# Gate weights of both layers and the context's output weights copied in memory, and loaded from the copies

## The chip, the cores and the metric

The kernel runs on one NeuronCore of one Trainium2 chip, in one launch. The metric is the device time in microseconds. A core has a matrix engine (TensorE, in the profile PE), a vector engine (DVE), a scalar engine (ACT), GpSimd (POOL) and a queue engine (SyncE, SP), which run side by side and meet at semaphores. 16 DMA engines move data between the device memory and the on-chip memory (SBUF). A transfer is issued by SP, ACT or POOL and is cut into packets, each a run of bytes that is contiguous on both sides. SP and ACT issue to hardware queues (q1 in the page), POOL to a software queue (q0).

## The reference

Two layers of a trunk over 256 latent tokens with 256 context tokens, width 1024, all in float32. What matters here:

```
pc = modulate(xc, norm1, sh1_c, sc1_c) @ w_in        # 6832 columns, the last 4096 of them gate logits
pl = modulate(xl, norm1, sh1_l, sc1_l) @ w_in
...                                                  # four mixers: two attentions, mLSTM, Hyena
def merge_branches(ys, gate_logits, w_branch, w_out):
    gl = gate_logits.reshape(B, L, N_BRANCH, -1)
    acc = sigmoid(gl[:, :, 0]) * (ys[0] @ w_branch[0])
    for i in range(1, N_BRANCH):
        acc = acc + sigmoid(gl[:, :, i]) * (ys[i] @ w_branch[i])
    return acc @ w_out
xl = xl + g1_l * merge_branches(..latents..)
xc = xc + g1_c * merge_branches(..context..)         # in the first layer alone
xc, xl = both + g2 * peer(modulate(both, norm2, ..)) # 8 heads x 16 of 16384 experts for each token
```

`w_in` and `w_out` are stored row by row, so a chunk of 256 columns is 1024 runs of 1 KB. The gate columns of one layer are 16 such chunks (16 MB), `w_out` is 4.

## The kernel before

The program is a row of stages with a barrier of all engines between them: `begin`, `opening` (line 2374), `experts_beside` (line 2489), `closing`, `experts` and `store`. `opening` does the first layer's context keys and the whole of its latent stream up to the residual. `experts_beside` does the first layer's experts for all 512 tokens, which fetch 128 rows of 4 KB from each of two tables for every token by indirect transfers that POOL issues, and weaves two strings of other work in between: first the context's own first layer (with its gates and its output product), then the second layer's latent projections, gates and Hyena. `closing` and `experts` finish the second layer.

A stage is a list of parts. A part has ticks, and in each tick methods for some engines (`sync` for SP, `tensor` for TensorE and so on). The stage's plan is one list of (part, tick); `perform` walks it once for each engine, so every engine runs its own instructions in the plan's order, and an instruction that waits holds up everything behind it on that engine. `braid` interleaves strings of ticks in proportion to their lengths.

`Gates` (line 1499) computes the gate logits: 32 tiles of 128 columns, two in a chunk. `Gates.load` (line 1518) is SP's load of chunk c into one of two ring buffers; from chunk 2 on it waits until TensorE is done with chunk c - 2 (`mult`). The tile's eight products stand at line 1556. `Branches` (line 1598) computes 32 steps of `ys @ w_branch`, two products each (line 1647), with eight chunks of 512 KB for four steps each, loaded at line 1616 two chunks ahead. `Merged` (line 1675) is the output product (line 1713) with four chunks of `w_out`, loaded at line 1691; its first two loads are issued at its first tick.

The second half of the opening's plan (lines 2421 to 2423; `g` are the gates' ticks, `b` the branches'):

```python
plan += braid(whole(attn), whole(conv), g[14:22])
plan += braid(whole(lstm), g[22:], b[:16])
plan += b[16:] + braid(whole(merged), whole(other))
```

Hyena's first tick (line 1387) makes SP load `k_dft` and the stored spectra, 1 MB each. Each kind of part has its own semaphores; transfers that SP issues go out in SP's order. In `experts_beside` the context's gates, its output product and the second layer's gates use a ring whose buffers are 256 columns wide, so that the eight pieces of a chunk lie one behind the other in each SBUF partition (8 KB).

Of the kernel before, what the change touches and what calls it, by code (L numbers as in the profile page):

```python
# [12 lines left out]
F32 = mybir.dt.float32  # L13
# [6 lines left out]
P = 128  # L20
D = 1024
KD = D // P
# [18 lines left out]
O_GATE = O_HY + 3 * HY_W  # L41
# [30 lines left out]
def sbuf(nc, name, shape, dtype):  # L72

    NUMBER[1] += 1
    return nc.sbuf_tensor(f"{name}_{NUMBER[1]}", shape, dtype)


class Chain:


    def __init__(self, eng, sem):
        self.eng, self.sem, self.n = eng, sem, 0
# [178 lines left out]
class Part:  # L261
# [3 lines left out]
    after = ()  # L265
# [5 lines left out]
    def sync(self, sp, i):  # L271
        pass
# [14 lines left out]
def whole(part):  # L287
    return [(part, i) for i in range(part.ticks)]


def braid(*strings):

    at = [((j + 0.5) / len(s), n, x) for n, s in enumerate(strings) for j, x in enumerate(s)]
    return [x for _, _, x in sorted(at, key=lambda a: a[:2])]
# [48 lines left out]
class Modulation(Part):  # L343
# [3 lines left out]
    STEPS = 9  # L347
# [1148 lines left out]
STEPS = [(i, k) for i in range(N_BRANCH) for k in range(KD)]  # L1496


class Gates(Part):
# [2 lines left out]
    LOT = 4  # L1502
    ticks = len(STEPS) + 2

    def __init__(self, nc, sems, m, w_in, f, ring, sig, banks, after, branches, room=None, flip=0, away=None):
        self.away = away
        self.room_for, self.flip = room if room else [after, after], flip
        self.nc, self.m, self.f, self.ring, self.sig, self.banks, self.after = nc, m, f, ring, sig, banks, after
        self.w = w_in.rearrange("(k p) n -> p k n", p=P)
        self.branches, self.room = branches, sig.shape[1]  # L1510
        self.mult, self.out, self.sigmoids, self.in0, self.in1, *self.stored = sems(
            "g_mult", "g_out", "g_sigmoids", "g_in0", "g_in1", *([f"g_stored{j}" for j in range(2)] if away is not None else []))
        self.ins = [self.in0, self.in1]
# [4 lines left out]
    def load(self, sp, c):  # L1518
        if c >= 2:
            sp.wait_ge(self.mult, 2 * (c - 1))  # L1520
        else:
            for sem, n in self.room_for[c]:
                sp.wait_ge(sem, n)
        at = O_GATE + 256 * c
        sp.dma_start(self.ring[:, (c + self.flip) % 2, :, 0:256], self.w[:, :, at:at + 256]).then_inc(self.ins[c % 2], 16)

    def sync(self, sp, i):
        if i == 0:
# [31 lines left out]
    def scalar(self, act, i):  # L1560
        nc, j, L = self.nc, i - 1, self.LOT
        if 0 <= j < len(STEPS):
            if j == 0:
                self.enter(act)
            act.wait_ge(self.mult, j + 1)
            if j >= self.room and self.away is None:
                act.wait_ge(self.branches.prod_done, j - self.room + 1)
            elif j >= self.room and j % self.LOT == 0:
                lot = (j - self.room) // self.LOT
                act.wait_ge(self.stored[lot % 2], 16 * (lot // 2 + 1))  # L1570
            nc.scalar.copy(self.sig[:, j % self.room, :], self.m.ps[:, self.banks[j % 2], 0:T]).then_inc(self.out, 1)  # L1571
        if i >= 2 and (i - 1) % L == 0:
            act.wait_ge(self.out, i - 1)
            at = (i - 1 - L) % self.room
            nc.scalar.activation(self.sig[:, at:at + L, :], self.sig[:, at:at + L, :], ACT.Sigmoid
                                 ).then_inc(self.sigmoids, 1)


class Fetched(Part):
# [95 lines left out]
class Merged(Part):  # L1675
# [1 line left out]

    ticks = KD + 1

    def __init__(self, nc, sems, m, mod, w_out, acc, ring, lo, banks, after, room):  # L1680
        self.nc, self.m, self.mod, self.acc, self.ring, self.lo, self.banks, self.after = (
            nc, m, mod, acc, ring, lo, banks, after)
        self.w = w_out.rearrange("(k p) n -> p k n", p=P)
        self.kind, self.room = (1 if lo < CTX else 0), room
        self.mult, self.out, *self.ins = sems("o_mult", "o_out", "o_in0", "o_in1")
        self.done = [(self.out, KD)]

    def load(self, sp, c):
        if c >= 2:
            sp.wait_ge(self.mult, 2 * (c - 1))  # L1690
        sp.dma_start(self.ring[:, c % 2, :, 0:256], self.w[:, :, c * 256:(c + 1) * 256]).then_inc(self.ins[c % 2], 16)

    def sync(self, sp, i):
        if i == 0:
# [679 lines left out]
def opening(nc, m, d, l, kv, spectra, rounds, front):  # L2374
# [3 lines left out]
    with sbuf(nc, "arena", [P, X + 12416 - FRONT], F32) as rest, sbuf(nc, "gbias", [1, T + 16], F32) as gbias:  # L2378
        arena = front, rest
        sems = Sems(nc)  # L2380
        f = front_memory(arena)
        vec, mod = m.vec[l], m.mod[l]
        ring, w_in = cut(arena, RING, 2, KD, 272), d["w_in"][l]
# [13 lines left out]
        side = Modulation(nc, sems, m, rounds, cut(arena, MODR, 2, 2, MROUND), cut(arena, MODR + 4096, MCH), 7)  # L2397
# [4 lines left out]
        attn = Attention(nc, sems, m, f, kv, 1, attention_memory(arena, X), (2, 3, 4), heads.done + heads_c.done)  # L2402
        conv = Hyena(nc, sems, m, vec, d, f, hyena_memory(arena, X + 2096, X + 4144), spectra, (5, 6, 7),
                     heads.done + rest1.done)
        lstm = Mlstm(nc, sems, m, vec, f, kv, 1, mlstm_memory(arena, X, NB), (2, 3, 4, 5), attn.done + conv.done)
        branch = Branches(nc, sems, m, d["w_branch"][l], f, cut(arena, MODR, 2, 2, 512), cut(arena, X + LSTM, KD, T),
                          cut(arena, X + LSTM + 2048, 2, T), (6, 7), attn.done + conv.done,
                          [attn.done, attn.done, lstm.done, conv.done], rest1.done)
# [4 lines left out]
                        [(branch.acc_done, len(STEPS)), (gates.mult, len(STEPS))] + lstm.done,  # L2413
                        [(gates.mult, len(STEPS))])
        other = Norm(nc, sems, m, mod, 0, 0, f.h, cut(arena, 2048, T), 4, merged.after, True)
        g, b, q = whole(gates), whole(branch), whole(side)
        plan = braid(whole(norm_c), q[:8])
        plan += whole(proj_c)[:1] + whole(Ahead(proj)) + braid(whole(proj_c)[1:], whole(norm), whole(filt), q[8:24])
        plan += braid(whole(heads_c), whole(proj), q[24:54])
        plan += braid(whole(heads), g[:14], q[54:]) + [(rest0, 0), (rest1, 0)]  # L2420
        plan += braid(whole(attn), whole(conv), g[14:22])
        plan += braid(whole(lstm), g[22:], b[:16])
        plan += b[16:] + braid(whole(merged), whole(other))
        perform(nc, sems, plan)


# [62 lines left out]
def experts_beside(nc, m, d, l, kv, spectra, sigs, front):  # L2489
# [3 lines left out]
    with ExitStack() as ctx:  # L2493
# [3 lines left out]
        sems = Sems(nc)  # L2497
        f = front_memory(arena)
# [11 lines left out]
        branch = Branches(nc, sems, m, d["w_branch"][l], f, cut(arena, 6144, 2, 2, 512), cut(arena, 4096, KD, T),  # L2510
                          cut(arena, Z + 7168, 2, T), (6, 7), conv.done, [[], [], [], []])
        gates = Gates(nc, sems, m, d["w_in"][l], f, cut(arena, Z, 2, KD, 256), cut(arena, Z + 4096, 12, T), (4, 5),
                      conv.done, branch)
        branch.gates = gates
        merged = Merged(nc, sems, m, mod, d["w_out"][l], branch.acc, cut(arena, Z, 2, KD, 256), 0, (4, 5),
                        [(branch.acc_done, len(STEPS)), (gates.mult, len(STEPS)), (gates.out, len(STEPS))],
                        [(gates.mult, len(STEPS))])
        norm2c = Norm(nc, sems, m, mod, 3 * KD, 0, h2, cut(arena, 2048, T), 6,
                      merged.done + [(peer.q_mult, 16), (peer.h_turned, 4)])
        peer.normed = [norm2l, norm2c]  # L2520
# [10 lines left out]
                            known, known)  # L2531
        heads_n = Heads(nc, sems, m, vec, d, l + 1, f, kv, 1, True, True, heads_memory(arena, Z), (6, 7), proj_n.done)
        gates_n = Gates(nc, sems, m, d["w_in"][l + 1], f, cut(arena, Z, 2, KD, 256), cut(arena, Z + 4096, 12, T), (4, 5),
                        heads_n.done, None, away=sigs)
        conv_n = Hyena(nc, sems, m, vec, d, f, hyena_memory(arena, 0, Z), spectra, (4, 5, 6),
                       [(gates_n.mult, len(STEPS)), (gates_n.out, len(STEPS))] + [
                           (gates_n.stored[j], 64) for j in range(2)])
# [19 lines left out]
def build(nc, d, out):  # L2557
    NUMBER[:] = [0, 0]
    m = Mem()
    kv = Mem()  # L2560
    with ExitStack() as ctx:
        sb = lambda name, shape: ctx.enter_context(sbuf(nc, name, shape, F32))
        m.ps = ctx.enter_context(nc.psum_tensor("ps", [P, BANKS, BANK], F32))
        m.sq = sb("squares", [P, C_N, P])
        m.resid = sb("resid", [P, KD, TOK])
        m.cond = sb("cond", [P, KD, 32])
        m.vec = [sb("vec", [P, V_ROWS]) for _ in range(LAYERS)]
        m.mod = [sb("mod", [P, 6 * KD, 2]) for _ in range(LAYERS)]
        m.products = [sb("mod_products", [P, 6 * KD, 2]) for _ in range(LAYERS)]
        m.eps = sb("eps", [P, 1])  # L2570
        kv.km, kv.vm = sb("km", [P, MLA_H, TOK]), sb("vm", [P, NB, MLA_H * MLA_V])
        kv.gk, kv.gv = sb("gk", [P, TOK]), sb("gv", [P, NB, P])
        kv.mk, kv.mv, kv.mg = sb("mk", [P, 2, TOK]), sb("mv", [P, NB, ML_H, HD + 1]), sb("mg", [P, NB, 4 * ML_H])
        spectra = nc.dram_tensor("spectra", (P, 4 * KF * HY_W), F32, kind="Internal").ap()
        begin(nc, m, kv, d)
        rounds = [(d["ada_w"][0], r * MROUND, m.products[0]) for r in range(2, 6)]
        rounds += [(d["ada_w"][1], r * MROUND, m.products[1]) for r in range(6)]
        sigs = nc.dram_tensor("sigs", (P, len(STEPS), T), F32, kind="Internal").ap()
        with sbuf(nc, "front", [P, FRONT], F32) as front:
            opening(nc, m, d, 0, kv, spectra, rounds, front)  # L2580
            experts_beside(nc, m, d, 0, kv, spectra, sigs, front)
            closing(nc, m, d, 1, kv, sigs, front)
        experts(nc, m, d, 1)
        store(nc, m, out)
# [99 lines left out]
```

## Time and profile before

| | |
|---|---|
| median of 3 runs | 3312.9 us (3311.84 to 3319.93) |
| the profiled execution | 3324.62 us, span 3322.7 us |
| TensorE, DVE, POOL, ACT busy | 2296.2, 1849.8, 1748.8, 617.3 us |
| moved | 1028.53 MB, mean 310 GB/s |
| software queue (q0), hardware queue (q1) | 847.35 MB and 179.15 MB, 66.8% and 16.1% of 16 engines' span |
| packets | 395065; under 2 KB 176283, under 8 KB 393755 |

The profile covers one execution. The span is from its first to its last instruction. The opening lasts until about 573 us, `experts_beside` until about 2310, `closing` until about 2570. A transfer's landing is counted from its issue by the queue's engine to the arrival of its last byte's semaphore. A queue's share is the time that its packets took, summed over 16 engines, over 16 times the stretch.

### The profile page before, as it was taken

How to read it: one execution, taken by the hardware profiler on the slowest of the kernel's cores; microseconds unless marked ns; L12 is line 12 of the kernel's file. 1: busy time of each engine (PE TensorE's matmuls, PEld its weight loads, DVE VectorE, ACT ScalarE, POOL GpSimd, SP SyncE). 2: the span in 40 equal slices, each digit the busy share in tenths (PEclk: the TensorE clock that was granted, in tenths of full speed). 3: DMA queues.
4: the chain of work that ended last, by engine and by line, in shares of the span. 5: the costliest groups of instructions: out<-in, count | busy, mean ns of one | idle time of the engine just before them, and what ended most of it. 6: DMA issues, size and time to landing. Idle time of an engine off the chain costs nothing. (4 is left out here: it accounts for less than half of the span.)

```text
span 3322.7 us, 31994 instructions
## 1 busy us (share of the span) xinstructions
PE 2296.2 (69%) x10877; PEld 1372.8 (41%) x10877; DVE 1849.8 (56%) x4792; ACT 617.3 (19%) x1252; POOL 1748.8 (53%) x1580
## 2 busy tenths in 40 slices
PE   5999999878857787566676477554798555444435
PEld 3676687734525555123443155321576322101001
DVE  1324334667775556767446945573334766666652
ACT  2113531124211121112102112210241111110000
POOL 0001000467675566777667666776000577777775
PEclk8999999877668898667888688866789766555555
DMA  8576223899999999999999999998303999999997
GB/s 293 178 266 236 88 64 105 298 335 382 333 379 337 350 391 368 383 385 352 349 349 384 334 354 396 401 386 332 113 7 113 307 387 405 403 386 383 395 367 312
DMA packets 395065, 1028.53 MB, mean 310 GB/s; under 512 B 31891, under 2 KB 176283, under 8 KB 393755
## 3 DMA queue, kind: packets, MB, share of 16 engines
q0 software_dynamic: 232064, 847.35, 66.8%
q1 hardware_dynamic: 162794, 179.15, 16.1%
q8 instruction: 89, 1.46, 0.2%
q14 instruction: 70, 0.57, 0.0%
q10 hardware_dynamic: 48, 0.01, 0.0%
HBM read 1019.05 MB, written 7.34 MB: 309 GB/s over the span
## 5 line engine op out<-in xcount | busy, mean ns | idle before, releaser
L1885 POOL DMA_INDIRECT expert_rows<-in_peer_u,chosen x768 | 867.2, 1129 | 850.1 <-DVE chosen L2241 576.8
L2133 DVE CUSTOM_DVE_ANT_0 expert_rows<-expert_rows,h_rows 128x1024 f32<-128x1024 f32 x768 | 935.9, 1222 | 554.6 <-DMA expert_rows<-in_peer_u,chosen 532.3
L1898 POOL DMA_INDIRECT expert_rows<-in_peer_v,row_of x768 | 852.5, 1110 | 410.9 <-PE ps L2025 210.3
L2025 PE MATMUL ps<-expert_rows,weights 128*32 128x512 f32 x3072 | 589.7, 849 | 685.4 <-DMA expert_rows<-in_peer_v,row_of 682.9
L2025 PEld LDWEIGHTS ps<-expert_rows,weights 128*32 128x32 f32 x3072 | 77.2, 125 | 963.3 <-issue 953.7
L1556 PE MATMUL ps<-front,arena 128*128 128x256 f32 x1536 | 384.8, 408 | 79.3 <-DMA arena<-in_w_in 78.5
L1556 PEld LDWEIGHTS ps<-front,arena 128*128 128x128 f32 x1536 | 308.7, 205 | 163.3 <-DMA arena<-in_w_in 63.9
L595 PE MATMUL ps<-front,arena 128*128 128x256 f32 (+1 forms) x816 | 201.9, 406 | 43.6 <-DMA arena<-in_w_in 39.5
L1953 PE MATMUL ps<-h,wq 128*128 128x256 f32 x768 | 200.4, 415 | 5.1 <-ACT h L439 3.7
L595 PEld LDWEIGHTS ps<-front,arena 128*128 128x128 f32 (+1 forms) x816 | 159.7, 199 | 89.2 <-issue 34.1
L361 POOL DMA_DIRECT2D arena<-in_ada_w x40 | 28.8, 719 | 285.0 <-PE ps L384 246.4
L1953 PEld LDWEIGHTS ps<-h,wq 128*128 128x128 f32 x768 | 155.7, 210 | 54.3 <-issue 30.6
L1571 ACT COPY arena<-ps 128x256 f32<-128x256 f32 x96 | 35.9, 373 | 330.7 <-PE ps L1556 330.7
L1647 PE MATMUL ps<-front,arena 128*128 128x256 f32 x256 | 65.0, 402 | 16.0 <-DVE arena L1663 12.4
L2098 ACT COPY weights<-ps 128x128 f32<-128x128 f32 x48 | 12.8, 266 | 337.7 <-DVE row_of L2176 266.9
L2076 ACT ACTIVATE gelu<-dots 128x16 f32<-128x16 f32 x48 | 10.4, 216 | 344.4 <-DVE dots L2133 344.2
L2058 ACT COPY scores<-ps 128x256 f32<-128x256 f32 x48 | 17.8, 372 | 297.3 <-PE ps L1967 297.3
L629 DVE COPY front<-ps 128x256 f32<-128x256 f32 (+2 forms) x28 | 11.8, 422 | 109.0 <-PE ps L595 99.6
L943 DVE TENSOR_REDUCE arena<-ps 128x1 f32<-128x512 f32 (+1 forms) x48 | 28.8, 600 | 74.3 <-PE ps L893 73.9
L831 DVE RECIPROCAL arena<-arena 96x512 f32<-96x512 f32 (+2 forms) x21 | 63.9, 3042 | 10.9 <-ACT arena L741 10.4
L2043 ACT COPY subkeysT<-ps 128x256 f32<-128x256 f32 x48 | 17.8, 371 | 266.9 <-PE ps L1932 266.9
L1186 DVE SCALAR_TENSOR_TENSOR arena<-arena,ps 128x256 f32<-128x256 f32 x80 | 25.5, 376 | 69.1 <-PE ps L1075 59.9
(356 smaller groups left out, 3185.6 us busy)
## 6 DMA issues: line engine op xcount, KB each, us to landing
arena<-in_w_in SPq DMA_DIRECT2D x79, 1024.0 KB, 13.5
arena<-in_ada_w POOLq DMA_DIRECT2D x40, 1024.0 KB, 6.5
wq<-in_peer_wq SPq DMA_DIRECT2D x48, 512.0 KB, 9.4
arena<-in_w_out SPq DMA_DIRECT2D x12, 1024.0 KB, 7.7
expert_rows<-in_peer_u,chosen POOLq DMA_INDIRECT x768, 6.6
expert_rows<-in_peer_v,row_of POOLq DMA_INDIRECT x768, 7.1
ada_w<-in_ada_w SPq DMA_DIRECT2D x4, 2048.0 KB, 23.0
arena<-in_w_branch SPq DMA_DIRECT2D x16, 512.0 KB, 3.5
```

What stands on the lines that cost most here:

```text
L361: pool.dma_start(self.raw[:, j % self.RING, :, :], weights.rearrange("(k p) n -> p k n", p=P)[:, k0:k0 + 2, lo:lo + MROUND]).then_inc(self ...
L595: ins = nc.tensor.matmul(m.ps[0:n, bank, 0:T], w, h[:, k, :], start=(k == 0), stop=(k == KD - 1))
L831: self.own.link(nc.vector.reciprocal(self.tile(x.rs2, j), self.tile(x.rs2, j)))
L943: self.own.link(nc.vector.reduce_max(x.st[:, 2, u:u + 1], m.ps[:, self.S, 0:n], axis=AX.X))
L1556: ins = nc.tensor.matmul(m.ps[:, self.banks[i % 2], 0:T], self.ring[:, (c + self.flip) % 2, k, (i % 2) * P:(i % 2 + 1) * P], self.f.h[:, k ...
L1571: nc.scalar.copy(self.sig[:, j % self.room, :], self.m.ps[:, self.banks[j % 2], 0:T]).then_inc(self.out, 1)
L1647: ins = nc.tensor.matmul(m.ps[:, self.bank(n), 0:T], self.wb[:, n // 4 % 2, a, (k % 4) * P:(k % 4 + 1) * P], self.f.yT[:, i, a, :], start= ...
L1885: nc.gpsimd.indirect_dma_start(x.ring[:, j % self.R, :], None, self.u_rows, bass.IndirectOffsetOnAxis(x.chosen[:, w, q:q + 1], 0)).then_in ...
L1898: nc.gpsimd.indirect_dma_start(x.ring[:, j % self.R, :], None, self.v_rows, bass.IndirectOffsetOnAxis(x.rows[:, w % 4, 4 * c + r:4 * c + r ...
L1953: ins = nc.tensor.matmul(m.ps[:, self.QB + c, 0:T], x.wq[:, b, part, k, c * P:(c + 1) * P], self.h[:, 4 * part + k, :], start=(part == 0 a ...
L2025: ins = nc.tensor.matmul(m.ps[to:to + 32, half, :], flat[:, r * P + 32 * c:r * P + 32 * c + 32], x.ring[:, self.place_of["v", a] % self.R, ...
L2133: nc.vector.tensor_tensor_reduce(u, u, x.ht, 1.0, 0.0, ALU.mult, ALU.add, x.dots[:, at:at + 1]).then_inc(self.u_dotted, 1)
```

## The change

A new part, `Relay`, issues on SP 36 copies from memory to memory: the 16 gate chunks of layer 0, the 4 chunks of layer 0's `w_out` and the 16 gate chunks of layer 1. Each copy reads a chunk as it lies in the weights (1024 runs of 1 KB) and writes it to a new tensor in device memory in which each partition's part of a chunk is 8 KB in one run. A copy waits for nothing; at the last tick SP waits until all 36 have landed. The ticks are braided into the second half of the opening: 18 with attention and Hyena, 10 with mLSTM, 8 with the last branch steps. In `experts_beside` the context's gates, its output product and the second layer's gates load from the new tensors. The opening's own gates and output product, and the closing's, load as before.

```diff
--- before.py
+++ after.py
@@ -1502,8 +1502,8 @@
     LOT = 4
     ticks = len(STEPS) + 2
 
-    def __init__(self, nc, sems, m, w_in, f, ring, sig, banks, after, branches, room=None, flip=0, away=None):
-        self.away = away
+    def __init__(self, nc, sems, m, w_in, f, ring, sig, banks, after, branches, room=None, flip=0, away=None, flat=None):
+        self.away, self.flat = away, flat
         self.room_for, self.flip = room if room else [after, after], flip
         self.nc, self.m, self.f, self.ring, self.sig, self.banks, self.after = nc, m, f, ring, sig, banks, after
         self.w = w_in.rearrange("(k p) n -> p k n", p=P)
@@ -1522,7 +1522,8 @@
             for sem, n in self.room_for[c]:
                 sp.wait_ge(sem, n)
         at = O_GATE + 256 * c
-        sp.dma_start(self.ring[:, (c + self.flip) % 2, :, 0:256], self.w[:, :, at:at + 256]).then_inc(self.ins[c % 2], 16)
+        weights = self.w[:, :, at:at + 256] if self.flat is None else self.flat[c]
+        sp.dma_start(self.ring[:, (c + self.flip) % 2, :, 0:256], weights).then_inc(self.ins[c % 2], 16)
 
     def sync(self, sp, i):
         if i == 0:
@@ -1574,6 +1575,24 @@
             at = (i - 1 - L) % self.room
             nc.scalar.activation(self.sig[:, at:at + L, :], self.sig[:, at:at + L, :], ACT.Sigmoid
                                  ).then_inc(self.sigmoids, 1)
+
+
+class Relay(Part):
+
+
+
+    LOTS = 4
+
+    def __init__(self, sems, copies):
+        self.copies, self.ticks = copies, len(copies)
+        self.copied = sems(*[f"copied{j}" for j in range(self.LOTS)])
+
+    def sync(self, sp, i):
+        to, src = self.copies[i]
+        sp.dma_start(to, src).then_inc(self.copied[i % self.LOTS], 16)
+        if i == self.ticks - 1:
+            for j in range(self.LOTS):
+                sp.wait_ge(self.copied[j], 16 * len(range(j, self.ticks, self.LOTS)))
 
 
 class Fetched(Part):
@@ -1677,7 +1696,8 @@
 
     ticks = KD + 1
 
-    def __init__(self, nc, sems, m, mod, w_out, acc, ring, lo, banks, after, room):
+    def __init__(self, nc, sems, m, mod, w_out, acc, ring, lo, banks, after, room, flat=None):
+        self.flat = flat
         self.nc, self.m, self.mod, self.acc, self.ring, self.lo, self.banks, self.after = (
             nc, m, mod, acc, ring, lo, banks, after)
         self.w = w_out.rearrange("(k p) n -> p k n", p=P)
@@ -1688,7 +1708,8 @@
     def load(self, sp, c):
         if c >= 2:
             sp.wait_ge(self.mult, 2 * (c - 1))
-        sp.dma_start(self.ring[:, c % 2, :, 0:256], self.w[:, :, c * 256:(c + 1) * 256]).then_inc(self.ins[c % 2], 16)
+        weights = self.w[:, :, c * 256:(c + 1) * 256] if self.flat is None else self.flat[c]
+        sp.dma_start(self.ring[:, c % 2, :, 0:256], weights).then_inc(self.ins[c % 2], 16)
 
     def sync(self, sp, i):
         if i == 0:
@@ -2413,14 +2434,14 @@
                         [(branch.acc_done, len(STEPS)), (gates.mult, len(STEPS))] + lstm.done,
                         [(gates.mult, len(STEPS))])
         other = Norm(nc, sems, m, mod, 0, 0, f.h, cut(arena, 2048, T), 4, merged.after, True)
-        g, b, q = whole(gates), whole(branch), whole(side)
+        g, b, q, c = whole(gates), whole(branch), whole(side), whole(Relay(sems, m.copies))
         plan = braid(whole(norm_c), q[:8])
         plan += whole(proj_c)[:1] + whole(Ahead(proj)) + braid(whole(proj_c)[1:], whole(norm), whole(filt), q[8:24])
         plan += braid(whole(heads_c), whole(proj), q[24:54])
         plan += braid(whole(heads), g[:14], q[54:]) + [(rest0, 0), (rest1, 0)]
-        plan += braid(whole(attn), whole(conv), g[14:22])
-        plan += braid(whole(lstm), g[22:], b[:16])
-        plan += b[16:] + braid(whole(merged), whole(other))
+        plan += braid(whole(attn), whole(conv), g[14:22], c[:18])
+        plan += braid(whole(lstm), g[22:], b[:16], c[18:28])
+        plan += braid(b[16:], c[28:]) + braid(whole(merged), whole(other))
         perform(nc, sems, plan)
 
 
@@ -2510,11 +2531,11 @@
         branch = Branches(nc, sems, m, d["w_branch"][l], f, cut(arena, 6144, 2, 2, 512), cut(arena, 4096, KD, T),
                           cut(arena, Z + 7168, 2, T), (6, 7), conv.done, [[], [], [], []])
         gates = Gates(nc, sems, m, d["w_in"][l], f, cut(arena, Z, 2, KD, 256), cut(arena, Z + 4096, 12, T), (4, 5),
-                      conv.done, branch)
+                      conv.done, branch, flat=m.flat[0])
         branch.gates = gates
         merged = Merged(nc, sems, m, mod, d["w_out"][l], branch.acc, cut(arena, Z, 2, KD, 256), 0, (4, 5),
                         [(branch.acc_done, len(STEPS)), (gates.mult, len(STEPS)), (gates.out, len(STEPS))],
-                        [(gates.mult, len(STEPS))])
+                        [(gates.mult, len(STEPS))], m.flat[1])
         norm2c = Norm(nc, sems, m, mod, 3 * KD, 0, h2, cut(arena, 2048, T), 6,
                       merged.done + [(peer.q_mult, 16), (peer.h_turned, 4)])
         peer.normed = [norm2l, norm2c]
@@ -2531,7 +2552,7 @@
                             known, known)
         heads_n = Heads(nc, sems, m, vec, d, l + 1, f, kv, 1, True, True, heads_memory(arena, Z), (6, 7), proj_n.done)
         gates_n = Gates(nc, sems, m, d["w_in"][l + 1], f, cut(arena, Z, 2, KD, 256), cut(arena, Z + 4096, 12, T), (4, 5),
-                        heads_n.done, None, away=sigs)
+                        heads_n.done, None, away=sigs, flat=m.flat[2])
         conv_n = Hyena(nc, sems, m, vec, d, f, hyena_memory(arena, 0, Z), spectra, (4, 5, 6),
                        [(gates_n.mult, len(STEPS)), (gates_n.out, len(STEPS))] + [
                            (gates_n.stored[j], 64) for j in range(2)])
@@ -2576,6 +2597,13 @@
         rounds = [(d["ada_w"][0], r * MROUND, m.products[0]) for r in range(2, 6)]
         rounds += [(d["ada_w"][1], r * MROUND, m.products[1]) for r in range(6)]
         sigs = nc.dram_tensor("sigs", (P, len(STEPS), T), F32, kind="Internal").ap()
+        m.flat = [[], [], []]
+        m.copies = []
+        for j, (w, at, n) in enumerate(((d["w_in"][0], O_GATE, 16), (d["w_out"][0], 0, 4), (d["w_in"][1], O_GATE, 16))):
+            flat = nc.dram_tensor(f"flat{j}", (n, P, KD * 256), F32, kind="Internal").ap()
+            for c in range(n):
+                m.flat[j].append(flat[c].rearrange("p (k n) -> p k n", k=KD))
+                m.copies.append((m.flat[j][c], w.rearrange("(k p) n -> p k n", p=P)[:, :, at + 256 * c:at + 256 * (c + 1)]))
         with sbuf(nc, "front", [P, FRONT], F32) as front:
             opening(nc, m, d, 0, kv, spectra, rounds, front)
             experts_beside(nc, m, d, 0, kv, spectra, sigs, front)
```

## Rows read from the trace of the kernel before

**Rows 1.** The page's slices: 40 equal parts of the span, busy tenths.

```profile
PE   5999999878857787566676477554798555444435
...
DMA  8576223899999999999999999998303999999997
```

**Rows 2.** Table by stretch, with granted clock, DMA share, GB/s.

```profile
core 0: us, PE busy (x) PEld busy (x) DVE busy (x) ACT busy (x) POOL busy (x), PEclk, DMA share, GB/s
330.00:560.00 230.00, 216.48 (x1097) 171.62 (x1098) 91.75 (x262) 83.49 (x170) 0.00 (x0) 0.97 0.25 80
...
1010.00:1330.00 320.00, 255.66 (x1195) 176.51 (x1195) 182.59 (x493) 56.12 (x98) 191.12 (x172) 0.88 0.98 364
...
1890.00:2150.00 260.00, 182.98 (x872) 119.51 (x872) 138.56 (x371) 49.23 (x83) 176.99 (x150) 0.85 1.00 379
...
1270.00:1290.00 20.00, 16.25 (x82) 10.62 (x80) 16.75 (x45) 1.66 (x2) 11.90 (x12) 0.99 1.04 395
```

**Rows 3.** Waits of 330 to 560 us on TensorE: us in total, times, longest.

```profile
PE ps L893 <- ACT arena L921: 4.8, 6, 1.9
```

**Rows 4.** DMA view of 1100 to 1330 us: packets, MB, share; issues to landing.

```profile
q1 hardware_dynamic: 18607, 19.53, 25.2%
...
arena<-in_w_in SPq DMA_DIRECT2D x10, 1024.0 KB, 17.4
```

**Rows 5.** DMA view of 2363 to 2372 us.

```profile
DMA packets 491, 3.63 MB, mean 403 GB/s; under 512 B 48, under 2 KB 48, under 8 KB 48
...
q1 hardware_dynamic: 491, 3.63, 98.6%
```

**Rows 6.** Waits in 1010 to 1335 and in 1890 to 2155 us, all engines.

```profile
PE ps L1556 <- DMA arena<-in_w_in: 32.8, 8, 12.8
...
PE ps L1556 <- DMA arena<-in_w_in: 45.7, 12, 15.4
```

**Rows 7.** DMA view of 333 to 338 us, 40 slices, 1 KB packets first.

```profile
GB/s 360 385 369 385 393 385 385 385 393 385 377 352 319 287 311 303 401 320 533 492 508 393 393 524 328 393 459 393 524 328 393 459 393 524 262 590 197 418 238 254
```

**Rows 8.** DMA view of 343 to 352 us: one load alone.

```profile
q1 hardware_dynamic: 1040, 1.05, 38.1%
...
arena<-in_w_in SPq DMA_DIRECT2D x1, 1024.0 KB, 5.2
```

**Rows 9.** The two loads of line 1691 between 530 and 533 us.

```profile
L1691 SPq DMA_DIRECT2D arena<-in_w_out x2: 469/526/582, 531.4 to 531.9; - x2
...
DMA to landing us min/median/max: 6.3/7.5/8.7
```

**Rows 10.** SP's timeline in the opening: start us, us, issue.

```profile
330.61 0.37 SPq L1387 DMA_DIRECT2D arena<-in_k_dft  x1
...
421.78 14.06 SPq L1525 DMA_DIRECT2D arena<-in_w_in  x2
...
523.74 0.37 SPq L1616 DMA_DIRECT2D arena<-in_w_branch  x1
...
531.43 26.40 SPq L1691 DMA_DIRECT2D arena<-in_w_out  x4
```

**Rows 11.** TensorE's timeline: start us, us, instructions, idle time before them.

```profile
423.31 1.10 PE L1647 MATMUL ps<-front,arena 128*128 128x256 f32 x4 [0.55 <-ACT front L934]
424.25 3.62 PE L1556 MATMUL ps<-front,arena 128*128 128x256 f32 x16
...
436.73 3.62 PE L1556 MATMUL ps<-front,arena 128*128 128x256 f32 x16
...
539.89 7.17 PE L1713 MATMUL ps<-arena 128*128 128x256 f32 x32 [0.97 <-DVE arena L1671]
546.90 3.62 PE L451 MATMUL ps<-front,squares 128*128 128x256 f32 x16
...
573.72 5.41 PE L451 MATMUL ps<-h,squares 128*128 128x256 f32 x16 [2.48 <-ACT h L432]
```
## The prediction

> **What bounds the kernel now.** I read the page's slices first, then a table by stage, the waits and SP's own timeline. The chain of waits covers only the last 10 us, since a barrier between stages cuts it, so each stage is read alone.
>
> In the slices [rows 1] TensorE is busy from 80 to about 580 us while the DMA digits fall to 1 and 2 between 330 and 580; after that the DMA digits are 9 up to 2300. The table [rows 2] makes it two regimes. From 330 to 560 us (the opening's second half) TensorE is busy 216.5 of 230 us and the DMA engines 0.25: TensorE sets the time there, and the largest of its waits sums to 4.8 us [rows 3]. A late load in this stretch is lost time. From 580 to 2300 us the DMA engines set the time: their digits are 9 nearly throughout [rows 1], the share is 0.98 and 1.00 in the two stretches that matter here, and 1.04 is what a full one shows [rows 2]. The 36 loads that the change redirects lie in two stretches of this regime: 16 gate and 4 output loads between 1010 and 1330, 16 gate loads between 1890 and 2150.
>
> **The gain: 36 loads with 8 KB runs.** In a full stretch the hardware queue's packets, nearly all 1 KB, take 25.2% of 16 engines over 230 us for 19.53 MB, which is 47.5 engine-us per MB [rows 4]; a 1.049 MB load thus costs 16 engines 3.11 us. The kernel already fetches one tensor in 8 KB runs: 98.6% of 16 engines over 9 us for 3.63 MB [rows 5], 39.1 engine-us per MB, 2.56 us a load. 36 x 0.55 = 19.8 us, and as the engines are full in both stretches I count all of it. It can't be below nothing, as the bytes are the same in fewer packets. The upper bound adds what the two stretches leave unused: (1.04 - 0.98) x 320 + (1.04 - 1.00) x 260 = 29 us [rows 2], if all of that comes of TensorE's waits for these loads, which are 32.8 and 45.7 us there [rows 6]: 49 us.
>
> A rule of the Trainium skill speaks against any gain: DMA: Bandwidth & Descriptors, Specifications, has the line rate reached from 512 B on, so that 1 KB runs lose nothing. The rows differ (3.11 against 2.56 us), so I hold to them; by the rule the change is all cost, a rival below.
>
> **The price of one copy.** 36 copies of 1.049 MB from memory to memory are added, cut to 1 KB on the reading side. No row shows such a transfer. From below: 1 KB loads one behind the other move at 385 GB/s [rows 7], 2.7 us each. From above: a lone load's engine time is 38.1% of 9 us = 3.43 us [rows 8]; a reading and a writing leg of that length, one after the other, make 6.9 us. Less than the lower end is excluded, since a copy reads the same 1 KB runs. I take 5.2 us: every byte crosses the memory twice, and the 8 KB stretch, with 403 GB/s among the fastest shown, moves twice 1.049 MB in 5.2 us [rows 5].
>
> The Trainium skill (DMA: Bandwidth & Descriptors, Latency and other measured facts) gives up to 214 GB/s each way for copies between memory tensors, an estimate of 4.9 us a copy. No row shows one. By it the opening's cost below is 51 us and the sum +32, 3345.
>
> **What the copies do to the opening.** They have no waits, so SP issues them as soon as it reaches them, and they stand in the same hardware queue as every weight load. I take that queue as first in, first out: two output-weight loads issued at 531.4 and 531.9 land after 6.3 and 8.7 us, so 2.9 us apart, not together [rows 9]. For a queued 1 KB load I take 2.9 us, between the 2.7 of [rows 7] and the 3.11 of [rows 4]; a lone one lands 5.2 us after issue [rows 8], which leaves 2.3 for issue and receipt.
>
> First part, braided with attention and Hyena: 18 copies. From 330.6 us SP issues k_dft (2.9 us), the spectra (2.6, 8 KB runs), gate chunks 8 to 11 (4 x 2.9) and then branch chunk 0 (1.5, half the size) [rows 10], and all 18 copies come before the branch chunk. SP reaches the copies long before TensorE needs them, so from 330 on the queue never runs dry: branch chunk 0 lands at 330.6 + 2.3 + 18.6 + 18c = 351.5 + 18c, c the price of a copy. TensorE needs it at 423.3 [rows 11]. At c = 5.2 it lands at 445.1: 21.8 us of stall. Behind that step stands all of TensorE's list, with mLSTM's products and the gates. The cover lasts up to c = 4.0. The gate chunks have fewer copies ahead of them: chunk 11, with 15, lands at 330.6 + 2.3 + 17.1 + 78 = 428 where its tile starts at 424.3 [rows 11], a delay that lies within the 21.8.
>
> Second part, with mLSTM: 10 copies over 90 us, at most three ahead of a load. Loads here have 15 to 30 us between issue and use (gate chunk 12: issued at 421.8 [rows 10], used at 436.7 [rows 11], and no copy stands between it and branch chunk 1). Nothing.
>
> Third part, with the branch steps 16 to 32: copies 28 to 35, two behind each of branch chunks 5 and 6, four behind chunk 7; then SP waits for all copies, and only then issues the first output weights. Branch chunk 5 is issued at 523.7 [rows 10]. The queue is then full: three branch chunks (4.5 us) and 8c, all landed at 523.7 + 2.3 + 4.5 + 8c = 530.5 + 8c; the output load lands 5.2 later. At c = 5.2: 577.3. TensorE began that product at 539.9 [rows 11]: 37.4 us lost, in three steps (branch step 24 and 28 late by one pair of copies each, the rest before the output product). Here nothing covers: in this part TensorE's list holds only branch steps, the output product and the next norm, all behind it, and DVE follows TensorE. What the old order had was an output load issued at 531.4 [rows 10], ahead of its use.
>
> After an idle TensorE the granted clock is lower for a while: 16 products took 5.41 us behind a gap of 2.48 us and 3.62 without one [rows 11]. That costs some 2 us after each of four stalls; against it stand the opening's small waits, about 5 us in the largest row [rows 3], which a stall absorbs. I set both to nothing.
>
> **Sum.** +21.8 + 37.4 - 19.8 = +39.4 us. The profiled execution takes 3324.6 us (span 3322.7), 11.7 us over the median of 3312.9; on it the sum is 3364.0, and as a median 3312.9 + 39.4 = 3352. In general the cost is 26c - 76 from c = 4.0 on, 8c - 4.2 below.
>
> **Rivals.**
> 1. Cheap copies: at c = 2.7 branch chunk 0 lands at 400, in time; the tail costs 17.4 us; with the gain -2.4: 3310, no change. It decides from c = 4.0 down. For it: no row shows that the memory, and not the engines, caps the rate. Against: it needs 2 x 1.049 MB in 2.7 us, 777 GB/s of memory traffic, and the 8 KB stretch shows 403 [rows 5].
> 2. Dear copies, c = 6.9: 52.4 + 51.0 - 19.8 = +83.6, 3397. It decides where the writing leg doesn't overlap the reading one. For it: the writes go to the same memory. Against: in a load the SBUF leg overlaps, or 2.56 us for 1 MB could not be.
> 3. The gate stretches gain 49 us because TensorE no longer waits for their weights and the unused DMA time fills: +10 with c = 5.2 (3323), -32 with c = 2.7 (3281): this is the faster side, and it decides where the copies are cheap. For it: 78 us of waits [rows 6]. Against: a share of 0.98 and 1.00; a row that comes sooner is a row less later.
> 4. Runs of 8 KB cost no less per byte, by the rule above, or the loads stay cut to 1 KB: no gain, +59, 3372.
>
> **How the numbers follow.** Forecast (c from 4.4 to 6.0, 3331 to 3373) 0.52; rival 1 0.22; rival 2 0.10; rival 3 0.10; rival 4 0.06. 0.3% is 10 us, about what a measurement of this kernel tells from no change. Faster: 0.07 of rival 1 and 0.05 of rival 3, 0.12. Same: 0.15 and 0.03, 0.18. The rest, 0.70, is slower. The range 3300 to 3392 leaves out the lowest of rivals 1 and 3 and the upper part of rival 2.
>
> **What would show it.** Right: a wait on branch weights of about 20 us near 423, one before the output product near 570, the DMA share of 330 to 560 near 0.8 or more, the barrier of the opening some 59 us later; from there to the end of the next stage about 20 us less, with the redirected loads landing well below the 17.4 us of before [rows 4]. Wrong: copies that take under 4 us each, so that the first wait is absent; or a stage with the expert rows that is shorter by more than 30 us.

## The result and the profile after

The changed kernel takes 3303.69 us in the median of 14 runs (3285.12 to 3312.73) against 3318.88 for the kernel before on the same chip; the ratio is 0.9936, interval 0.9913 to 0.9958, 14 to 29 us faster. The forecast was 39 us slower. The profiled execution takes 3306.0 us, its span 3304.2.

In the page's slices the three DMA digits between 330 and 580 us are 9, 5 and 5 where they were 2, 2 and 3 [rows 1]; the row by stretch says the same of 330 to 560: TensorE busy 203.8 us for 216.5, at a granted clock of 0.93 for 0.97, the DMA share 0.70 for 0.25 [rows 2].

```profile
PE   5999997877867888466767578655798555444435
...
DMA  7577955699999999999999999998302999999997
```

```profile
330.00:560.00 230.00, 203.81 (x1014) 158.45 (x1012) 90.21 (x259) 83.54 (x171) 0.00 (x0) 0.93 0.70 229
```

**The copies.** A stretch of 40 us in which nine copies and two gate loads are issued, the queue full throughout:

```profile
DMA packets 13104, 13.25 MB, mean 331 GB/s; under 512 B 198, under 2 KB 13101, under 8 KB 13101
...
q1 hardware_dynamic: 13101, 13.21, 103.2%
...
flat<-in_w_in SPq DMA_DIRECT2D x9, 1024.0 KB, 12.5
```

331 GB/s, so 1.049 MB in 3.17 us: this is c, forecast at 5.2. Two of the eleven transfers are plain loads; from 382 to 394 us the queue holds copies alone:

```profile
DMA packets 4026, 4.07 MB, mean 339 GB/s; under 512 B 63, under 2 KB 4025, under 8 KB 4025
...
q1 hardware_dynamic: 4025, 4.06, 104.2%
```

That is 3.1 us a copy. Each byte is read and written, so 678 GB/s cross the memory. The price is that of a plain load: 104.2% of 16 engines over 12 us for 4025 packets is 49.7 ns of engine time a packet, and the 1 KB loads of before took 49.8 (25.2% over 230 us for 18607 packets [rows 4]). A copy lands 12.5 us after its issue, four times 3.1: some three others stand ahead of it in the queue.

SP's issues in the opening, and TensorE's steps that wait for them (starting times and lengths; the idle time before a step and what ended it in brackets):

```profile
332.91 0.37 SPq L1387 DMA_DIRECT2D arena<-in_k_dft  x1
...
404.45 3.43 SPq L1635 DMA_DIRECT2D arena<-in_w_branch  x2
...
529.35 0.37 SPq L1635 DMA_DIRECT2D arena<-in_w_branch  x1
529.76 1.36 SPq L1592 DMA_DIRECT2D flat<-in_w_in  x2
533.17 1.49 SPq L1635 DMA_DIRECT2D arena<-in_w_branch  x1
534.70 4.59 SPq L1592 DMA_DIRECT2D flat<-in_w_in  x2
539.33 3.54 SPq L1635 DMA_DIRECT2D arena<-in_w_branch  x1
542.91 9.73 SPq L1592 DMA_DIRECT2D flat<-in_w_in  x4
561.82 26.39 SPq L1712 DMA_DIRECT2D arena<-in_w_out  x4
```

```profile
430.48 1.10 PE L1666 MATMUL ps<-front,arena 128*128 128x256 f32 x4 [0.55 <-ACT front L934]
...
542.71 5.24 PE L1666 MATMUL ps<-front,arena 128*128 128x256 f32 x16 [6.08 <-DMA arena<-in_w_branch]
549.80 3.72 PE L1666 MATMUL ps<-front,arena 128*128 128x256 f32 x16 [1.85 <-DMA arena<-in_w_branch]
567.53 9.92 PE L1734 MATMUL ps<-arena 128*128 128x256 f32 x32 [14.01 <-DMA arena<-in_w_out]
...
604.13 5.26 PE L451 MATMUL ps<-h,squares 128*128 128x256 f32 x16 [2.50 <-ACT h L432]
```

The two loads issued at 404.45, branch chunks 0 and 1, land like this:

```profile
DMA to landing us min/median/max: 9.9/10.6/11.2
```

Chunk 0 has landed by 415.7 and is in time: its step starts at 430.5, with the same 0.55 us of idle time as before and no DMA named [rows 11]. The tail goes as forecast: the output loads are issued at 561.8 in place of 531.4 [rows 10], and TensorE waits 6.1, 1.9 and 14.0 us, 21.9 in all. After the long wait 32 products take 9.92 us; they took 7.17 [rows 11]. The stage's end is read from the last norm's products: 604.1 for 573.7 [rows 11], 30.4 us later. 2.3 of them lie ahead of Hyena's first loads: SP issues `k_dft` at 332.9 for 330.6 [rows 10]. Another 4.9 lie between that issue and the first branch step (97.6 us for 92.7), where TensorE waits for no weight. They go with the granted clock, and the clock was the same in a kernel without copies (1 KB loads, below, where this part takes 97.7 us); before, after, and that kernel:

```profile
333.00:423.00 90.00, 82.29 (x413) 59.60 (x411) 30.92 (x80) 45.50 (x100) 0.00 (x0) 1.00 0.25 80
...
333.00:423.00 90.00, 82.49 (x386) 59.05 (x387) 31.44 (x82) 45.30 (x98) 0.00 (x0) 0.94 0.89 292
...
333.00:423.00 90.00, 82.53 (x387) 59.19 (x387) 31.29 (x82) 45.46 (x98) 0.00 (x0) 0.94 0.25 82
```

In the last two the granted clock falls to half (1.2 GHz) twice, near 375 us behind a gap of 1.9 us and near 420 behind one of 1.4, for 10.2 us in all; the trace of before has the same gaps and no fall. So these 4.9 us are scatter between executions and no price of the copies. 23.2 us are left.

**The two stretches with the loads from the copies.** SP's first redirected loads and the first issues behind each stretch, before:

```profile
1020.71 1.00 SPq L1525 DMA_DIRECT2D arena<-in_w_in  x2
...
1343.55 0.32 SPq L1255 DMA_DIRECT2D front<-in_k_feat  x1
...
1895.49 0.99 SPq L1525 DMA_DIRECT2D arena<-in_w_in  x2
...
2145.17 0.38 SPq L1387 DMA_DIRECT2D front<-in_k_dft  x1
```

and after:

```profile
1044.26 0.81 SPq L1526 DMA_DIRECT2D arena<-flat  x2
...
1342.64 0.32 SPq L1255 DMA_DIRECT2D front<-in_k_feat  x1
...
1893.97 0.82 SPq L1526 DMA_DIRECT2D arena<-flat  x2
...
2131.00 0.38 SPq L1387 DMA_DIRECT2D front<-in_k_dft  x1
```

The first stretch is 298.4 us long for 322.8, the second 237.0 for 249.7: 37.1 us less. What the queues took in them (packets, MB, share of 16 engines; windows of 322 and 250 us before, of 297 and 237 after), before:

```profile
q0 software_dynamic: 24937, 90.80, 73.4%
q1 hardware_dynamic: 25664, 27.00, 24.9%
...
q0 software_dynamic: 20202, 73.59, 75.6%
q1 hardware_dynamic: 18880, 21.50, 24.4%
```

and after:

```profile
q0 software_dynamic: 25006, 91.05, 77.7%
q1 hardware_dynamic: 7744, 27.00, 23.2%
...
arena<-flat SPq DMA_DIRECT2D x20, 1024.0 KB, 8.4
...
q0 software_dynamic: 20224, 73.66, 78.4%
q1 hardware_dynamic: 4544, 21.50, 22.5%
```

Share times length gives the engine time. The hardware queue: 80.2 to 68.9 and 61.0 to 53.3 us, 19.0 less. The rows' queue, with the same 45,000 packets: 236.3 to 230.8 and 189.0 to 185.8, 8.7 less. So a packet of the rows took less time too. The rest of the 38 us by which these windows shrank is time in which the engines had not been full: the shares sum to 1.01 and 1.01 for 0.98 and 1.00. A redirected load lands in 8.4 us for 17.4 [rows 4], and TensorE's waits for gate weights are these, for 32.8 and 45.7 [rows 6]:

```profile
PE ps L1557 <- DMA arena<-flat: 8.4, 1, 8.4
...
PE ps L1557 <- DMA arena<-flat: 8.3, 1, 8.3
```

### The profile page after: what moved, and what is told of

Its sections match the earlier page's. It is cut to its first block and busy times, and to the rows that moved or that the text cites. A ratio compares the mean times of both kernels' runs of the same rounds, so it can differ in the third digit from the quotient of the medians.

```text
span 3304.2 us, 32032 instructions
## 1 busy us (share of the span) xinstructions
PE 2282.7 (69%) x10877; PEld 1363.8 (41%) x10877; DVE 1849.1 (56%) x4792; ACT 617.2 (19%) x1252; POOL 1728.1 (52%) x1580
## 5 line engine op out<-in xcount | busy, mean ns | idle before, releaser
L1906 POOL DMA_INDIRECT expert_rows<-in_peer_u,chosen x768 | 848.6, 1105 | 880.1 <-DVE chosen L2262 605.0
L1557 PE MATMUL ps<-front,arena 128*128 128x256 f32 x1536 | 370.2, 396 | 17.4 <-DMA arena<-flat 16.7
L1557 PEld LDWEIGHTS ps<-front,arena 128*128 128x128 f32 x1536 | 299.7, 199 | 96.8 <-issue 48.7
L1666 PE MATMUL ps<-front,arena 128*128 128x256 f32 x256 | 67.5, 412 | 23.9 <-DVE arena L1682 12.9
L629 DVE COPY front<-ps 128x256 f32<-128x256 f32 (+2 forms) x28 | 11.8, 422 | 108.8 <-PE ps L595 95.1
L1734 PE MATMUL ps<-arena 128*128 128x256 f32 x256 | 58.7, 393 | 15.0 <-DMA arena<-in_w_out 14.0
```

The costliest lines, as they stand in the source:

```text
L1557: ins = nc.tensor.matmul(m.ps[:, self.banks[i % 2], 0:T], self.ring[:, (c + self.flip) % 2, k, (i % 2) * P:(i % 2 + 1) * P], self.f.h[:, k ...
L1666: ins = nc.tensor.matmul(m.ps[:, self.bank(n), 0:T], self.wb[:, n // 4 % 2, a, (k % 4) * P:(k % 4 + 1) * P], self.f.yT[:, i, a, :], start= ...
L1734: ins = nc.tensor.matmul(m.ps[:, self.banks[k % 2], 0:T], self.ring[:, c % 2, j, (k % 2) * P:(k % 2 + 1) * P], self.acc[:, j, :], start=(j ...
L1906: nc.gpsimd.indirect_dma_start(x.ring[:, j % self.R, :], None, self.u_rows, bass.IndirectOffsetOnAxis(x.chosen[:, w, q:q + 1], 0)).then_in ...
```

## The experiments

All edits are against the changed kernel, that of the two queues against the kernel before. Theory A: run length is what counts in the stretches, and the 37 us are real; theory B: only 20 us are, the rest is the scatter of one execution. For the opening: the loads stand behind the copies in one queue; the rival is that SP's wait costs the time.

**Copies alone.** The three `flat` arguments in `experts_beside` are taken out; the copies stay, unused.

```diff
-                      conv.done, branch, flat=m.flat[0])
+                      conv.done, branch)
-                        [(gates.mult, len(STEPS))], m.flat[1])
+                        [(gates.mult, len(STEPS))])
-                        heads_n.done, None, away=sigs, flat=m.flat[2])
+                        heads_n.done, None, away=sigs)
```

> Copies as in the changed kernel, all later loads from the weights as before. The profile of the changed kernel has the opening's end 28 us later. If that is all the copies cost, this is the kernel before plus 28 us (26 to 32), ratio 1.0085. If the copies also cost something later, or the 37 us that the two gate stretches gain are partly scatter between executions, it lies elsewhere: under +20 or over +36.

Measured: ratio 1.0070 (1.0043 to 1.0097), 23 us slower of 3323.16 (14 to 32). TensorE's waits on weights between 330 and 600 us (total, times, longest):

```profile
PE ps L1734 <- DMA arena<-in_w_out: 14.0, 1, 14.0
PE ps L1666 <- DMA arena<-in_w_branch: 5.8, 2, 4.2
```

The same wait before the output product, the sum 19.8 us. The copies cost what the opening shows: 23 us by the runs, and 23.2 of the 30.4 once the scatter ahead of the copies' waits is taken off.

**Loads alone, in runs of 8, 4, 2 and 1 KB.** No copies. The 36 loads take 1 MB each from the expert table `peer_u`, the same place for each run length, so that gates and output product get other numbers than the reference's. (For 8 KB, two rows of the table are joined in place of one being divided.)

```diff
+        R = 2048 // RUNS                       # RUNS = 1, 2, 4, 8: runs of 8, 4, 2, 1 KB
+            runs = d["peer_u"][layer].rearrange("e (b n) -> (e b) n", b=D // R)
+            for c in range(first, first + n):
+                m.flat[j].append(runs[c * P * RUNS:(c + 1) * P * RUNS].rearrange("(a p) n -> p a n", p=P))
...
+            to = to.rearrange("p (a k) n -> p a (k n)", a=RUNS)
```

> No copies; the 36 loads are taken from the expert table in 8 KB runs (other numbers than the gate and output weights, the same bytes and runs). Theory A (8 KB loads save 20 us of packet time, shorten the row packets beside them and let the rows run on, 37 us in all): kernel before minus 37 (30 to 45), ratio 0.989. Theory B (only the 20 us of packet time, the rest is scatter of one execution): minus 15 to 22, ratio 0.994.

> No copies, loads from the same places of the expert table as with 8 KB runs, in 4 KB runs. By packet time alone (168 ns for 4 KB, 316 for 8 KB, 48.7 for 1 KB: 2.69, 2.53, 3.12 us a load) three quarters of the 8 KB gain of 50 us, minus 36; by landing (16 packets per engine in turn with the rows' 4 KB packets, some 6 us against 4 and 14) nearly all, minus 42 to 50.

> The same in 2 KB runs. By packet time (87 ns for 2 KB: 2.78 us a load) 58% of the 8 KB gain, minus 28; by landing (32 packets in turn with the rows', some 8 us) about 55 to 60% as well, minus 25 to 30. Under minus 15 would say that only runs as long as the rows' own packets count.

> As the loads from the expert table, from the same places, but cut to 1 KB runs. If the run length is what counts (both theories): the kernel before, within 5 us, ratio 1.000. If it is where the weights lie in memory (a pitch of 27 KB between runs): the same gain as with 8 KB runs.

| runs | ratio (interval) | us | landing, median us | the two stretches, us |
|---|---|---|---|---|
| 8 KB | 0.9848 (0.9804 to 0.9893) | -51 | 8.5 | 530.2 |
| 4 KB | 0.9880 (0.9841 to 0.9919) | -40 | 9.9 | 540.3 |
| 2 KB | 0.9920 (0.9894 to 0.9947) | -27 | 12.0 | 548.9 |
| 1 KB | 1.0001 (0.9974 to 1.0028) | 0 | 17.2 | 575.3 |

The last column is the length of the two stretches together in the one profile of each, from the same two issues of SP as above. The other profiles say how far to trust it. With 1 KB runs from the weights it is 572.5 before, 570.0 with the copies alone and 575.6 with the copies of long runs below; with 8 KB runs it is 535.4 in the changed kernel and 529.3 and 535.6 in the two versions below that keep its loads. Profiles of one run length lie within 7 us, and the two run lengths are 34 to 46 apart.

Theory B falls: the gain is 36 to 65 us by the runs, with its middle above theory A's 30 to 45. Reading other places in memory with 1 KB runs changes nothing beyond 9 us either way; the run length counts. The doublings bring 27, 13 and 11 us. The first is clear of noise; the last two are not each by themselves, as the intervals overlap, but both together, from 2 to 8 KB, are. For 4 KB the two forecasts (36, and 42 to 50) are not told apart. With the copies alone, +23 - 51 = -28 us, and the whole change has -21 (14 to 29 less): the parts add up within their intervals.

**Two queues.** The kernel before, 1 KB runs, but half of each gate load from chunk 2 on is issued by ACT.

```diff
-            pe.wait_ge(self.ins[c % 2], 16 * (c // 2 + 1))
+            pe.wait_ge(self.ins[c % 2], (32 if self.split else 16) * (c // 2 + 1))
...
+            if self.split and i % 2 == 0 and i // 2 + 1 < len(STEPS) // 2:
+                self.piece(act, i // 2 + 1, KD // 2, KD)
```

> The kernel before, no copies, 1 KB runs, but from chunk 2 on half of each gate load of the second stage is issued on ACT's queue, so that it lands in about 10 us in place of 17 while its packets cost the engines the same. If the early landing is worth the part of the gain that packet time doesn't explain: minus 8 to 17 us, ratio 0.996. If only packet time counts: no change, within 4 us.

Measured: ratio 0.9970 (0.9943 to 0.9997), -10 us (1 to 19 less). TensorE's waits in the two stretches, and SP's issues at their ends:

```profile
PE ps L1564 <- DMA arena<-in_w_in: 18.7, 4, 14.6
...
PE ps L1564 <- DMA arena<-in_w_in: 14.9, 1, 14.9
```

```profile
1018.38 6.35 SPq L1533 DMA_DIRECT2D arena<-in_w_in  x4
...
1336.70 0.32 SPq L1255 DMA_DIRECT2D front<-in_k_feat  x1
...
1891.56 1.77 SPq L1533 DMA_DIRECT2D arena<-in_w_in  x3
...
2144.80 0.38 SPq L1387 DMA_DIRECT2D front<-in_k_dft  x1
```

The waits for gate weights fall from 78.5 to 33.6 us, but the stretches are 318.3 and 253.2 us long, 571.6 together for 572.5, and 570.0 to 575.6 is what 1 KB runs show anyway. In this profile, then, most of this waiting was worth nothing by itself; the runs leave it between 1 and 19 us. It is the smaller part of the 8 KB gain, and how much smaller stays open.

**The wait later.** SP's wait for all copies moves behind the output loads, to the end of the stage (`Landed` is that wait as a part of its own).

```diff
-        if i == self.ticks - 1:
-            for j in range(self.LOTS):
-                sp.wait_ge(self.copied[j], 16 * len(range(j, self.ticks, self.LOTS)))
...
-        plan += braid(b[16:], c[28:]) + braid(whole(merged), whole(other))
+        plan += braid(b[16:], c[28:]) + braid(whole(merged), whole(other)) + whole(Landed(relay))
```

> As the changed kernel, but SP's wait for all copies stands at the end of the stage, behind the output loads. Theory queue: the output loads still stand behind eight copies in the same queue, so they land at most 3 us sooner; the kernel before minus 21 to 25, as the changed kernel within 4 us. Theory wait: it is SP's wait that costs the 14 us before the output product; 14 us less than the changed kernel, before minus 35.

Measured: ratio 0.9933 (0.9905 to 0.9961), as the changed kernel. The waits:

```profile
PE ps L1744 <- DMA arena<-in_w_out: 11.5, 1, 11.5
PE ps L1676 <- DMA arena<-in_w_branch: 7.8, 2, 5.8
```

Without SP's wait the output product still waits 11.5 us, 2.5 less. It is the place in the queue that costs.

**Copies earlier.** No copies beside the last branch steps; the wait at the end.

```diff
-        plan += braid(whole(attn), whole(conv), g[14:22], c[:18])
-        plan += braid(whole(lstm), g[22:], b[:16], c[18:28])
+        plan += braid(whole(attn), whole(conv), g[14:22], c[:20])
+        plan += braid(whole(lstm), g[22:], b[:16], c[20:] + [(Part(), 0)] * 6)
+        plan += b[16:] + braid(whole(merged), whole(other)) + whole(Landed(relay))
```

> 20 copies with attention and Hyena, 16 in the first 70% of mLSTM's part, none with the last branch steps, the wait at the end of the stage. By the copy's measured 3.1 us all fit under TensorE's work: branch chunk 0 lands at 351.5 + 20 x 3.1 = 414, before 423. The opening ends where it did before, so the cost of 23 to 28 us goes and the gain stays: kernel before minus 40 to 50, ratio 0.986. If the copies slow the opening in another way than by late loads, half of the cost or more stays: minus 25 to 35.

Measured: 3283.16 us for 3322.53, ratio 0.9881 (0.9846 to 0.9917), -40 us (28 to 51 less). What is left of TensorE's waits on weights between 330 and 580, and the table's row:

```profile
PE ps L1676 <- DMA arena<-in_w_branch: 1.0, 1, 1.0
```

```profile
330.00:560.00 230.00, 216.29 (x1088) 170.46 (x1087) 91.79 (x263) 83.75 (x171) 0.00 (x0) 0.96 0.73 238
```

TensorE is busy 216.3 of 230 us as before [rows 2], beside the copies. The opening's last norm starts at 577.7; in the six profiles of kernels whose opening has no copies it starts between 573.2 and 580.7. By the ratio to the kernel before, this version is faster than the changed kernel too: 0.9881 for 0.9936, with intervals that overlap only from 0.9913 to 0.9917.

**Copies of long runs.** As the copies alone, but from the expert table, contiguous on both sides.

```diff
-                m.copies.append((m.flat[j][c], w.rearrange("(k p) n -> p k n", p=P)[:, :, at + 256 * c:at + 256 * (c + 1)]))
+                m.copies.append((m.flat[j][c], runs[c * P:(c + 1) * P]))
```

> As with the copies alone, but each copy reads 1 MB of the expert table in 8 KB runs (nothing uses the copies), so that both of its sides are 8 KB runs. If the DMA engines' packet time sets a copy's price, as the 3.1 us with 1 KB runs say, it is about 2.5 us (316 ns a packet), 410 to 420 GB/s each way, twice that over the memory, and the opening ends 4 to 5 us sooner than with 1 KB runs. If the memory, crossed twice, sets it, it stays at 3.1 us or more.

The experiment did not test what it was meant to, as the copies were not cut to 8 KB. Two stretches of the opening, the first without a load and with a queue that runs empty towards its end, the second with one gate load among copies:

```profile
DMA packets 107, 2.97 MB, mean 270 GB/s; under 512 B 61, under 2 KB 61, under 8 KB 61
...
DMA packets 1163, 5.05 MB, mean 361 GB/s; under 512 B 77, under 2 KB 1101, under 8 KB 1101
```

In the first, some 45 packets above 512 B carry 2.97 MB: the transfer is cut to 64 KB packets, not 8. In the second the rate is 361 GB/s, 2.9 us for 1 MB. The load's 1.05 MB of the 5.05 are only read, so some 650 GB/s cross the memory. 2.5 us is not reached, and the one run (3342.31 us) shows no sooner end of the opening (604.4 us, 599.1 with the copies alone). It does show again that both ways together pass 403 GB/s by far.

## Why the prediction was wrong

**The step that failed: "I take 5.2 us".** I held the traffic over the memory, both ways together, to the highest rate that the rows showed. Those rows were loads, in which the DMA engines set the rate; nothing in them spoke of the memory's own limit. A copy goes at 331 to 339 GB/s each way, 3.1 to 3.2 us, within the bounds I had set (2.7 to 6.9) and at most 17% above their lower end. Its packets take as much engine time as those of a 1 KB load, 49.7 and 49.8 ns: the price to take was the 3.11 us that stands in the prediction's own first sum, and the writing leg added no engine time to it. Rival 1 had named the point, c = 4.0; the case is rival 1 with part of rival 3. Both signs that the prediction gave for being wrong came: copies under 4 us with no first wait, and over 30 us less in the stretches of the expert rows. The Trainium skill's figure (DMA: Bandwidth & Descriptors, Latency and other measured facts, up to 214 GB/s each way, for tiles of 128 x 16 KiB) differs from this trace as well, 339 GB/s; the measurement decides.

**First part of the opening.** At c = 3.17 the formula gives 351.5 + 57 = 409 for branch chunk 0; it landed at 415.6, still ahead of its step. 2.3 of the 7 us are the later start. The rest contradicts "from 330 on the queue never runs dry": SP waited for a free gate buffer and issued chunk 11 only at 399.2, after the queue had run out. The term of 21.8 us vanished.

**Third part.** Right in mechanism and size: 8c - 4.2 is 21.2 us, the waits are 21.9. From the issue of branch chunk 5 to that of the output loads the formula has 2.3 + 4.5 + 8c = 32.2 us, and SP took 32.5 (529.35 to 561.82). That the waits come of the queue's order is shown by the wait moved later (11.5 of 14.0 us stay) and by the copies moved earlier (1.0 us of waits is left).

**The clock, set to nothing.** Of the 23.2 us that the copies cost in the profile, 21.9 are waits. 2.75 more are the slower products after the long wait, and 1.5 those after the first (16 in 5.24 us where 3.72 is seen after the second). The granted clock is 0.69 from 567 to 577 us and 0.68 from 542 to 548, a mean of its two levels, 1.2 and 2.4 GHz, and 1.00 in the stretches that follow. Against them stand 1.8 us of small waits of the old order (0.8 for a branch weight, 1.0 for DVE) that the long ones absorb. That is 24.4 for 23.2: setting both to nothing cost the sum some 2.5 us.

**The gain.** The step "36 x 0.55 = 19.8 us" is confirmed as packet time: 19.0 us of the hardware queue's engine time went. It was not the whole gain, 37 us in the profile and 36 to 65 in the loads alone. Missing were 8.7 us of engine time on the rows' packets and some 10 us in which the engines had not been full; the prediction had the second as an upper bound of 29 us in rival 3, and nothing for the first. So the gain was the second term that was mis-sized, 19.8 us for 37 (34 to 46 between all the profiles). Rival 3's reason for it, TensorE's waits, is not shown: with most of them gone by the two queues the stretches hardly shrank. What else left the engines not full stays open. Rival 4 falls. With it falls, for this kernel, the Trainium skill's rule (DMA: Bandwidth & Descriptors, Specifications) that the line rate is reached from 512 B on: the series gains from 1 to 2 KB and again from 2 to 8 KB.

**The sum.** In the profiles +30.4 at the opening's end, -37.1 in the two stretches, and -11.8 elsewhere, in work that the change doesn't touch (the span is 18.5 us less). The last lies within the scatter: behind the second stretch alone all eleven profiles do the same work, and take 1155 to 1197 us for it. The sum by the measured terms, +23 from the copies and -51 from the loads, is -28; by the medians it is -15, by the ratio -21. A slip of reading without consequence: the prediction has the DMA digits between 330 and 580 us fall to 1 and 2, and they are 2, 2 and 3.

## What to carry to other kernels

Where the DMA engines are full, a load's run length is time: 36 MB read in 8 KB runs in place of 1 KB were worth 1.5% here. Making the runs by a copy cost nothing beyond the noise (40 us gained with the early copies, 51 by the loads alone, intervals 28 to 51 and 36 to 65) where an earlier stage had idle DMA engines and no load with little slack stood behind the copies. A transfer that waits for nothing still costs through its place in the queue. A rate seen in transfers of one kind bounds those of another only if a row shows what sets it.

## What the runs showed of the hardware

- Memory to memory at 331 to 339 GB/s each way with 1 KB runs, 86 to 88% of the 385 GB/s of loads in a row [rows 7], and 49.7 ns of engine time for a 1 KB packet as in a load. TensorE beside it was busy 37.7 of the 40 us from 355 to 395, the same as before and as with the 1 KB loads and no copies.
- Packets of 4 KB took less engine time where the other queue's were 8 KB than where they were 1 KB: 236.3 us for 24,937 packets before and 230.8 for 25,006 after in the first stretch, 2.6% less a packet, and 1.8% less in the second.
- A copy that is contiguous on both sides was cut to packets of 64 KB (45 packets for 2.95 MB).
